# A hybrid decoder step on one core: in the last stage the eight samples come behind the four prompt tiles in place of ahead of them

## The reference

```python
D_MODEL, SEQ, DEC_BATCH, D_PLE = 1024, 512, 8, 256

def rmsnorm(x, g):
    y = x * lax.rsqrt(jnp.mean(x * x, axis=-1, keepdims=True) + EPS)
    return y * g

def trunk_layer(x, p_i, lw, conv_buf, attend):
    ...
    x = x + hier_moe(rmsnorm(x, lw['g_ffn']), ...)            # two experts a token, weighted
    gate = jax.nn.sigmoid(rmsnorm(x, lw['g_ple']) @ lw['w_ple_gate'])
    x = x + (p_i @ lw['w_ple']) * gate
    ...
# for the prompt (512 rows) and for the samples (8 rows) alike:
y = rmsnorm(x, g_final)
```

## Time and profile before

| | |
|---|---|
| time, median of 3 runs | 1018.1 us (1015.02 to 1021.15) |
| the profiled execution | 1013.72 us |
| its span | 1011.9 us |
| mean granted clock of TensorE | 0.919 of full speed |
| busy share of the span: PE, PEld, DVE, ACT, POOL | 85%, 44%, 34%, 19%, 26% |

### The profile page before, as it was taken

The page is one execution under the profiler, slowest core; times in us unless marked ns, Lnnn a source line. Parts: engine busy times, 40 slices in busy tenths (PEclk is TensorE's granted clock), DMA queues, the critical chain, the costliest instruction groups (busy, mean ns, idle before and its releaser), DMA issues.

```text
span 1011.9 us, 11581 instructions
## 1 busy us (share of the span) xinstructions
PE 857.7 (85%) x4281; PEld 445.9 (44%) x4281; DVE 348.3 (34%) x710; ACT 196.2 (19%) x395; POOL 262.1 (26%) x342
## 2 busy tenths in 40 slices
PE   5999877988999997699999677878788778984994
PEld 3888655655663545344433233333333333331441
DVE  5799967427425566231000000000000000002652
ACT  3110234433232120122111101010110101101431
POOL 6989866222310000211111111010111111001110
PEclk9999978998999997699999889998897989997998
DMA  9899955369976225399999999999999999997111
GB/s 305 320 345 374 328 216 207 142 235 387 371 280 272 84 104 221 120 408 410 416 400 402 411 388 420 402 413 405 419 406 416 391 404 410 427 403 305 58 42 42
DMA packets 53835, 316.47 MB, mean 313 GB/s; under 512 B 11247, under 2 KB 24111, under 8 KB 33049
## 3 DMA queue, kind: packets, MB, share of 16 engines
q1 hardware_dynamic: 34736, 233.28, 57.7%
q0 software_dynamic: 14480, 76.17, 19.8%
q10 hardware_dynamic: 4576, 6.46, 1.8%
HBM read 309.31 MB, written 14.82 MB: 320 GB/s over the span
## 4 chain that ended last, share of the span: by engine, by line
PE 30%; DMA 27%; DVE 1%; issue 1%; SPq 0%; ACT 0%; POOL 0%; POOLq 0%; DVEq 0%; ACTq 0%
DMA arena<-in_w_up 25%; PE psum L1680 16%; PE psum L1797 5%; PE psum L1695 3%; PE psum L1649 1%; DMA arena<-in_w_down 1%; PE psum L1671 1%; DMA moe_rows<-arena,indices 1%; PE psum L488 1%; PE psum L1688 0%; SPq L585 0%; DVE arena L2428 0%; PE psum L1780 0%; PE psum L1526 0%; DMA arena<-h_rows,indices 0%
## 5 line engine op out<-in xcount | busy, mean ns | idle before, releaser
L1680 PE MATMUL psum<-arena 128*64 128x512 f32 x1024 | 261.9, 670 | 67.2 <-DMA arena<-in_w_up 67.2
L1680 PEld LDWEIGHTS psum<-arena 128*64 128x64 f32 x1024 | 87.3, 153 | 217.3 <-issue 216.5
L2394 DVE TENSOR_TENSOR arena<-arena,psum 64x512 f32<-64x512 f32 x32 | 22.1, 692 | 371.2 <-ACT arena L1131 371.2
L1695 PE MATMUL psum<-arena 128*64 128x512 f32 x512 | 115.8, 592 | 1.9 <-DMA arena<-in_w_down 1.9
L1280 PE MATMUL psum<-arena 128*128 128x260 f32 x384 | 86.5, 388 | 0.0
L724 POOL TENSOR_TENSOR arena<-arena 128x2048 f32<-128x2048 f32 x18 | 81.6, 4540 | 0.9 <-DMA arena<-in_cache_k,indices 0.6
L1362 PE MATMUL psum<-arena 128*128 128x260 f32 x320 | 78.5, 398 | 2.5 <-DVEq L1961 2.5
L793 POOL COPY indices<-row_list 128x1 int32 (+1 forms) x26 | 4.6, 178 | 292.9 <-ACT arena L1137 292.9
L1280 PEld LDWEIGHTS psum<-arena 128*128 128x128 f32 x384 | 73.9, 193 | 12.3 <-issue 0.8
L1131 ACT ACTIVATE arena<-psum 64x512 f32<-64x512 f32 x32 | 18.9, 590 | 307.8 <-PE psum L1680 307.8
L1869 DVE TENSOR_REDUCE arena<-arena 128x32 f32<-128x2048 f32 x32 | 72.0, 2280 | 4.6 <-POOL arena L724 3.5
(11 more groups left out here) (331 smaller groups left out, 862.6 us busy)
## 6 DMA issues: line engine op xcount, KB each, us to landing
arena<-in_w_down SPq DMA_DIRECT2D x32, 2048.0 KB, 25.3
arena<-in_w_gate SPq DMA_DIRECT2D x31, 2048.0 KB, 18.5
arena<-in_w_up SPq DMA_DIRECT2D x31, 2048.0 KB, 23.0
arena<-in_w_in SPq DMA_DIRECT2D x11, 1024.0 KB, 9.4
arena<-in_x_prompt SPq DMA_DIRECT2D x8, 512.0 KB, 6.4
arena<-in_w_ple_gate SPq DMA_DIRECT2D x1, 4096.0 KB, 24.6
arena<-moe_rows SPq DMA_DIRECT2D x4, 1024.0 KB, 8.5
out<-arena ACTq DMA_DIRECT2D x8, 256.0 KB, 4.4
```

What stands on the lines that cost most here:

```text
L1680: last = mm(bank(s)[m * SLOTS:(m + 1) * SLOTS, :], hgT[s][:, k, :], w_gu[s][m][:, k, :], start=(k == 0), stop=(k == DC - 1))
L1695: last = mm(bank(6 + s)[n * SLOTS:(n + 1) * SLOTS, :], actT[s][:, k, :], w_dn[s][:, k, n * BANK:(n + 1) * BANK], start=(k == 0), stop=(k = ...
```

## The change

`LAST` becomes 0, 1, 2, 3, `QT`. On PE the samples' transposes stand in the middle of the first half of prompt tile 3 and their sums, in one piece of 16 matmuls, behind tile 3. On DVE `sum_parts` moves from ahead of the loop to the fifth position. Loads, stores, POOL's roots and ACT's steps follow `LAST`. No arithmetic changes.

```diff
--- before.py
+++ after.py
@@ -81,7 +81,7 @@
 GV_STEP = {3: 0, 4: 1, 6: 2, 7: 3, 8: 4}
 SPREADS = [("ck", 0), ("ck", 1)] + [x[1] for x in sorted([(s, ("ck", h)) for h, s in CK_STEP.items()]
                                                         + [(s, ("gv", t)) for s, t in GV_STEP.items()])]
-LAST = [QT] + list(range(QT))
+LAST = list(range(TILES))
 TURN = (0, 1, 2, QT, 3)
 POS = {t: n for n, t in enumerate(TURN)}
 H2_BUF = {0: 0, 1: 1, 2: 0, QT: 1, 3: 2}
@@ -1781,22 +1781,21 @@
                     last.then_inc(xT_full, 1)
 
             transpose_x(0)
-            pe.wait_ge(xT_ready, 2)
-            sample_sums(mm, bank(0), xT[0], w_gate_ple, range(DC // 2))
-            transpose_x(1)
-            sample_sums(mm, bank(0), xT[0], w_gate_ple, range(DC // 2, DC)).then_inc(pg_full, 2)
-            for i in range(1, TILES):
+            for i in range(QT):
                 for n in range(2):
                     if i >= 2:
                         pe.wait_ge(pg_sig, 2 * (i - 2) + n + 1)
                     for k in range(DC):
                         if n == 0 and k % 4 == 0:
                             pe.wait_ge(xT_ready, 2 * i + k // 4 + 1)
-                        if (n, k) == (0, DC // 2) and i + 1 < TILES:
+                        if (n, k) == (0, DC // 2):
                             transpose_x(i + 1)
                         last = mm(bank(2 * (i % 2) + n), xT[i % 2][:, k, :], w_gate_ple[:, k, n * BANK:(n + 1) * BANK],
                                   start=(k == 0), stop=(k == DC - 1))
                     last.then_inc(pg_full, 1)
+            pe.wait_ge(xT_ready, 2 * TILES)
+            pe.wait_ge(pg_sig, 2 * (QT - 2) + 2)
+            sample_sums(mm, bank(2 * (QT % 2)), xT[QT % 2], w_gate_ple).then_inc(pg_full, 2)
 
 
         @block.vector
@@ -2479,10 +2478,11 @@
             scale_xT(1)
             add_experts(2)
             dve.wait_ge(gfin_in, 16)
-            sum_parts(0)
             for n in range(TILES):
                 if 1 <= n < TILES - 1:
                     scale_xT(n + 1)
+                if n == QT:
+                    sum_parts(n)
                 add_gated(n, 0)
                 scale_x4(n)
                 if n >= 1 and n + 2 < TILES:
```

## The result

The changed kernel took 1026.74 us, median of 6 runs (1023.62 to 1029.71), against 1017.93 us of 6 runs of before: 1.0081 times as long, 95% interval 1.0058 to 1.0104, or 5.9 to 10.6 us. The profiled execution took 1026.47 us.

What follows compares the result with a forecast made beforehand. It took the last stage to be bound by PE's four prompt tiles, then the last tile's tail and POOL's DRAIN. Terms -3.85 + 1.2 + 0.7 + 11.06 = +9.1 us, on an average of 1017.0, gave 1026 us, range 1020 to 1032.

Steps and rivals of the forecast that it cites:

- The front: Start of the last stage: tile 0 loaded first, so PE's first gate matmul comes 3.85 us earlier (bounds -4.0 and -3.4).
- The clock: PE's first gate matmuls: they meet the low clock of 1.2 GHz, costing +1.2 us (0.7 to 2.4).
- the first two cases: PE's clock rises at 938.35 or at 940.2, losing 0.7 or 1.6 us on the gate's matmuls.
- the second and the third: PE's clock rises at 940.2 or at 941.85, losing 1.6 or 2.4 us on the gate's matmuls.
- PE's stream: PE in tile 3: the samples' transposes come into the stream, costing +0.7 us (0.3 to 1.0).
- The sums behind tile 3: The samples' sums on PE run under tile 3's tail on the other engines and cost nothing.
- The samples' chain: Behind tile 3: the samples' dependent steps, with no PE work left to cover them, move POOL's last root by +11.06 us.
- The closing: End of the kernel: POOL's DRAIN, 9.27 us, moves along with POOL's last root, adding 0.
- rival 1: End of the kernel: the DRAIN does not move along, the end falls to SP; +3.1 us, within 0.5%; chance 0.11.
- Rival 2: Last stage's start: clock low for longer, or first gate matmul no earlier than 937.4; +11 to +12 us; chance 0.10.
- Rival 3: Last stage's start: tile 0's load gains more, clock rises before the first gate matmul; +6.9 us; chance 0.07.
- POOL's last root near 1013: Sign in the changed kernel's profile: POOL's last root near 1013, its DRAIN of about 9 us from there.

Runs made afterwards that it cites:

- e7: Changed kernel with the samples' second sigmoid ahead of their first square in ACT's program; one run, 1025.14 us.
- e10: Changed kernel with the last position's root (the samples') on DVE, two refinements, POOL ending a tile earlier; 1.0036 times before.
- e12: Changed kernel with 16 filling matmuls, read by nobody, on PE ahead of tile 0's transposes; 1.0082 times before.
- e6: Kernel with the samples third, between prompt tiles 1 and 2, and DVE adding tile 3's experts ahead of the samples' sums; 1.0035 times before.
- e2: Kernel before, with one small POOL operation added that waits for both last stores; 1.0057 times before.
- e3: Kernel before, with the last tile's root moved from POOL to DVE, three refinements; 0.998 times before.
- e1: Changed kernel's samples moved to third position, between prompt tiles 1 and 2; 1.0101 times before.
- e5: Changed kernel with 12 filling matmuls, read by nobody, on PE ahead of tile 0's transposes; 1.0114 times before.
- e9: Changed kernel with 14 filling matmuls, read by nobody, on PE ahead of tile 0's transposes; 1.0105 times before.

## Why the prediction was right

The way, the size and the mechanism were right: 1026.74 us where 1026 was forecast, with a difference of 8.8 us (1026.74 - 1017.93) for a sum of 9.1. That it came within 0.7 us is luck: the base of 1017.0 was 0.9 low, and the runs of either kernel lie 6 us apart. The terms can be checked one by one in S, in the two profiled executions.

- *The front*, -3.85: measured 9.59 - 13.27 = -3.68. The load landed as estimated; the add of tile 1 began 0.15 us behind that of tile 0 and did not wait for its load.
- *The clock*, +1.2: measured 5.63 - 3.63 = +2.0, within the bounds of 0.7 to 2.4. I had taken a rise between the first two cases; it came 3.9 us into the gate's matmuls, between the second and the third. In e7 and e10, with the same program up to there, the term was 1.4 and 1.3: it changes by 0.7 us from one execution to another, and how close the +1.2 comes depends on the execution. e12, where this time goes to 3.70 us with the clock held up, shows that the clock is the whole of it.
- *PE's stream*, +0.7: +0.7 (0.59 for the samples' transposes, the rest in the other pieces of the chain). The front, the clock and this leave -1.0 at PE's end of tile 3, not -1.95.
- *The sums behind tile 3*, 0: PE had them done at 1003.88, 1.3 us ahead of ACT's first copy.
- *The samples' chain*, +11.06: 14.54 - 3.49 = +11.05. This is the term that decides, and e6 shows its cause: with the chain beside other tiles' matmuls S is 6.7 us shorter for the same work, though the sums then stand in PE's stream. The exact hit hides two errors of 0.3 us that cancel: the copies began 4.89 us behind PE's end of tile 3, not 5.21, and POOL's root came 9.65 us behind them, not 9.32. In the fifth position POOL's root begins 0.5 us behind ACT's square in both kernels (1002.13 behind 1001.62 before, 1014.88 behind 1014.37 now); for tile 3 in the fourth it was 0.16 (1003.49 behind 1003.33). So that delay goes with the position; the prediction had it in tile 3's tail. What makes it no run shows.
- *The closing*, 0: DRAIN of 9.25 against 9.27 us, at POOL's last root in both. e2 and e3 show that it moves with POOL's last instruction, which excludes rival 1. That rival's limit for the DRAIN, 5.3 us, was wrong by its own figures: from the DRAIN's start at 1002.4 + 9.1 = 1011.5 to the landing at 1014.9 are 3.4 us. Nothing hangs on it.
- *Rival 2* did not come about: the first gate matmul, 9.59 us into S, stands at 937.1 on the scale of before, not at 937.4 or later, and the sum stayed under 11. The clock alone went its way. *Rival 3* fell.

Sum: -3.68 + 2.0 + 0.7 + 11.05 = +10.1, the measured S; the forecast was 1.0 less, nearly all of it the clock. One of the signs named, POOL's last root near 1013, did not follow from the sum, which puts it at 1002.13 + 9.1 = 1011.2; on that scale it came at 1012.2.

## What to carry to other kernels

A short piece of work with a long chain of dependent steps belongs where something long runs beside it. Here a step on 8 rows cost as much as one on 128 (the sigmoid 0.72 us against 0.70), so at the end of the kernel the whole chain is seen, and ahead of the long work only its first part: the samples' adds and sums, which put PE's first gate matmul 3.7 us later. In the middle the chain is hidden only if no in-order engine has the next tile's work queued behind it (4.6 us in e1), and even so e6 stayed 3.4 us over before. And the last instruction on POOL was part of the end here: with the last root off POOL the closing behind the last store's issue took 3.3 us in place of 8.0 (e3).

## What the hardware showed

POOL's closing DRAIN ended 8.7 us behind the end of POOL's last instruction (before: 1003.03 to 1011.7), also where that instruction came long before the end (e3: 995.77 to 1004.5). In e2, where POOL had waited 3.5 us for the store, it was 8.9 (1013.48 to 1022.4). What it does in that time no run shows.

PE's clock fell in e5 and in e9 after PE had stood still for 2.2 and 2.1 us, with PE at work again: in e5 during the transposes, in e9 with the gate's matmuls already under way. In e12 PE stood still for 0.4 us there, and the clock did not fall.
